# Each 1 MB weight chunk as two transfers on their own semaphores, in a two-block transformer kernel

## The reference, cut to what matters

```python
for l in range(2):                                  # first block
    x = x + hybrid_layer(x, ...)                    # rmsnorm -> h @ w_in[l] (1024 x 3488) -> MLA attention,
                                                    # short conv, spatial gate, block attention -> y @ w_out[l]
for l in range(2):                                  # second block
    x = x + hybrid_mixer(rmsnorm(x), ...)           # h @ w_in (1024 x 2048), pooling and dilated attention, @ w_out
    if l == 0: x = x + swiglu(rmsnorm(x), wg, wu, wd)        # d_ff = 2816
    else:      x = x + moe_swiglu(rmsnorm(x), w_router, ...) # 8 experts, top 2, d_ff = 3584 each
return rmsnorm(x)
```

## Time and profile before

| | us |
|---|---|
| median of three runs | 1853.41 |
| the profiled execution's own time | 1849.0 |
| its span, first to last instruction | 1847.2 |
| PE busy | 1682.5 (91% of the span) |
| DVE busy | 1357.5 (73%) |
| ACT busy | 1055.2 (57%) |
| DMA queue of SP (q1) | 454.32 MB, 69.0% of 16 engines' span |

### The profile page before, as it was taken

The page is one execution under the profiler, slowest core; times in us unless marked ns, Lnnn a source line. Parts: engine busy times, 40 slices in busy tenths (PEclk is TensorE's granted clock), DMA queues, the critical chain, the costliest instruction groups (busy, mean ns, idle before and its releaser), DMA issues.

```text
span 1847.2 us, 21996 instructions
## 1 busy us (share of the span) xinstructions
PE 1682.5 (91%) x7707; PEld 1378.7 (75%) x7707; DVE 1357.5 (73%) x1456; ACT 1055.2 (57%) x976; POOL 18.6 (1%) x34
## 2 busy tenths in 40 slices
PE   5787977896999998669999999999999999999995
PEld 4666866775788886568888878888888888788884
DVE  4855765645644564568888888899888888888886
ACT  4333444353444445227767677777677776776773
POOL 1001000000000000000000000000000000000000
PEclk9997998897999999779999999999999999999997
DMA  9423532341544554128999999999999999999992
GB/s 320 160 91 97 175 122 69 113 144 46 160 159 146 197 189 158 51 87 307 361 369 354 345 338 366 372 355 362 326 347 366 369 362 341 345 366 367 356 348 111
DMA packets 153627, 462.59 MB, mean 250 GB/s; under 512 B 7806, under 2 KB 12172, under 8 KB 153404
## 3 DMA queue, kind: packets, MB, share of 16 engines
q1 hardware_dynamic: 151120, 454.32, 69.0%
q0 software_dynamic: 1696, 5.08, 1.0%
q10 hardware_dynamic: 716, 1.85, 0.3%
HBM read 460.18 MB, written 1.05 MB: 250 GB/s over the span
## 4 chain that ended last, share of the span: by engine, by line
PE 79%; DVE 10%; issue 4%; ACT 3%; DVEq 2%; DMA 1%; ACTq 0%; SPq 0%
PE ps L1875 15%; PE ps L1877 15%; PE ps L1876 15%; PE ps L1506 8%; PE ps L1508 8%; PE ps L1507 8%; PE ps L1902 2%; DVE actv_sb L1458 2%; DMA raw_sb<-w_in 1%; PE ps L1531 1%; PE ps L1809 1%; DVE wlo_sb L850 1%; ACT whi_sb L595 1%; ACT whi_sb L602 1%; PE ps L1823 1%
## 5 line engine op out<-in xcount | busy, mean ns | idle before, releaser
L857 DVE TENSOR_TENSOR wlo_sb<-raw_sb,whi_sb 128x2048 fp32r<-128x2048 f32 x336 | 766.4, 2291 | 131.8 <-ACT whi_sb L602 130.8
L602 ACT ACTIVATE whi_sb<-raw_sb 128x2048 fp32r<-128x2048 f32 x336 | 643.6, 1918 | 271.4 <-PE ps L1877 271.4
L850 DVE TENSOR_TENSOR wlo_sb<-raw_sb,whi_sb 128x1024 fp32r<-128x1024 f32 (+2 forms) x198 | 225.5, 1181 | 178.3 <-ACT whi_sb L595 176.2
L1875 PE MATMUL ps<-whi_sb,xlo_sb 128*128 128x512 f32 x896 | 352.5, 393 | 3.9 <-DVE wlo_sb L857 1.7
L1877 PE MATMUL ps<-whi_sb,xhi_sb 128*128 128x512 f32 x896 | 349.1, 390 | 0.0
L1876 PE MATMUL ps<-wlo_sb,xhi_sb 128*128 128x512 f32 x896 | 348.8, 389 | 0.0
L595 ACT ACTIVATE whi_sb<-raw_sb 128x1024 fp32r<-128x1024 f32 (+2 forms) x198 | 192.1, 1020 | 253.6 <-PE ps L1508 239.4
L1506 PE MATMUL ps<-whi_sb,xlo_sb 128*128 128x512 f32 (+2 forms) x672 | 269.5, 401 | 22.9 <-DVE xlo_sb L895 6.1
L1507 PE MATMUL ps<-wlo_sb,xhi_sb 128*128 128x512 f32 (+2 forms) x672 | 262.8, 391 | 0.0
L1508 PE MATMUL ps<-whi_sb,xhi_sb 128*128 128x512 f32 (+2 forms) x672 | 262.4, 391 | 0.0
L1875 PEld LDWEIGHTS ps<-whi_sb,xlo_sb 128*128 128x128 f32 x896 | 168.2, 188 | 40.9 <-DVE wlo_sb L857 3.7
(11 more groups left out here) (299 smaller groups left out, 1321.8 us busy)
## 6 DMA issues: line engine op xcount, KB each, us to landing
raw_sb<-moe_wg SPq DMA_DIRECT2D x115, 1024.0 KB, 6.1
raw_sb<-moe_wu SPq DMA_DIRECT2D x112, 1024.0 KB, 6.3
raw_sb<-moe_wd SPq DMA_DIRECT2D x112, 1024.0 KB, 6.5
raw_sb<-w_in SPq DMA_DIRECT2D x40, 1024.0 KB, 5.1
raw_sb<-w_out SPq DMA_DIRECT2D x16, 1024.0 KB, 5.0
raw_sb<-ffn_wg SPq DMA_DIRECT2D x10, 1024.0 KB, 5.1
raw_sb<-ffn_wu SPq DMA_DIRECT2D x10, 1024.0 KB, 5.1
raw_sb<-ffn_wd SPq DMA_DIRECT2D x10, 1024.0 KB, 5.0
```

The costliest lines, as they stand in the source:

```text
L602: nc.scalar.activation(whi[i % SPLIT][:, :, :], raw[i % RAW][:, :, :], ACT.Copy).then_inc(hi_ready, 2)
L850: op = V.tensor_tensor(wlo[i % SPLIT][:, c:c + k // 2, 0:n], raw[i % RAW][:, c:c + k // 2, 0:n], whi[i % SPLIT][:, c:c + k // 2, 0:n], ALU ...
L857: V.tensor_tensor(wlo[i % SPLIT][:, :, :], raw[i % RAW][:, :, :], whi[i % SPLIT][:, :, :], ALU.subtract).then_inc(lo_ready, 1)
L1875: mm(out, lo, whi[q % SPLIT][:, w, :], start=first, stop=False)
```

## The change

Every chunk is now fetched by two DMAs of half the row tiles each (two row tiles of 512 columns, or one of 1024 columns; one of 512 for the last chunks of the dense feed-forward's down projection). There are twelve semaphores instead of six, one for each half of each buffer. SP waits once for the buffer and then issues both halves back to back. In `act_hi` the wait for `split_used` now comes first, and then ahead of each half copy a wait for that half's semaphore. `act_hi_whole` waits for both halves, then for `split_used`, and copies the chunk whole as before. Nothing of DVE's or PE's program is changed.

```diff
-        raw_landed = [sem(f"raw_landed{i}") for i in range(RAW)]
+        raw_landed = [sem(f"raw_landed{i}_{c}") for i in range(RAW) for c in range(2)]
...
                 sp.wait_ge(lo_ready, number(c0, i - RAW + 1, per, l))
-            sp.dma_start(wide(raw[i % RAW]) if chunk.n == WIDE else raw[i % RAW][:, 0:chunk.k, 0:chunk.n],
-                         src(chunk.k0 * PART, chunk.k * PART, chunk.n0, chunk.n)).then_inc(raw_landed[i % RAW], 16)
+            dst = wide(raw[i % RAW]) if chunk.n == WIDE else raw[i % RAW][:, 0:chunk.k, 0:chunk.n]
+            half = chunk.k // 2
+            for c in (0, half):
+                sp.dma_start(dst[:, c:c + half, :], src((chunk.k0 + c) * PART, half * PART, chunk.n0, chunk.n)).then_inc(
+                    raw_landed[2 * (i % RAW) + (1 if c else 0)], 16)
...
-            act.wait_ge(raw_landed[i % RAW], landed(c0, i, per, l))
             if not (isinstance(l, int) and c0 + i + per * l < SPLIT):
 
                 act.wait_ge(split_used, number(c0, i - SPLIT + 1, per, l))
             for c in range(0, k, k // 2):
-
+                act.wait_ge(raw_landed[2 * (i % RAW) + (1 if c else 0)], landed(c0, i, per, l))
                 nc.scalar.activation(whi[i % SPLIT][:, c:c + k // 2, 0:n], raw[i % RAW][:, c:c + k // 2, 0:n],
                                      ACT.Copy).then_inc(hi_ready, 1)
...
-            act.wait_ge(raw_landed[i % RAW], landed(AT_MOE, i, PER, l))
+            for c in range(2):
+                act.wait_ge(raw_landed[2 * (i % RAW) + c], landed(AT_MOE, i, PER, l))
             act.wait_ge(split_used, number(AT_MOE, i - SPLIT + 1, PER, l))
```

## The result

| | before | after |
|---|---|---|
| median of 13 runs each, us | 1851.48 | 1858.42 |
| lowest to highest, us | 1844.83 to 1856.52 | 1854.41 to 1862.63 |
| profiled execution / its span, us | 1849.0 / 1847.2 | 1854.41 / 1852.6 |

The changed kernel is slower: ratio 1.0036, 95% interval 1.0027 to 1.0045. The prediction was 1852.3 us (1847.3 to 1857.0), no change. It was wrong in its sign and its range.

What follows compares the result with a forecast made beforehand. The prediction took PE to bound the expert stage (busy 99.5%), with weights waited for only at the start. A 1.14 us gain there and costs of 0 elsewhere gave 1853.41 - 1.14 = 1852.3 us, range 1847.3 to 1857.

Steps and rivals of the forecast that it cites:

- Where the change can act: Whole kernel: ACT waits for transfers in three copies only, 14.2 us, in the first 27 us; a gain only there.
- The start, 1.14 us: Third chunk at the start: DVE subtracts its first half earlier, ends at 29.14 not 30.28; PE's third chunk at 32.94.
- its second chunk would start 1.15 us earlier: PE at the start: DVE ends the second chunk at 26.42 with halves, so PE starts and finishes it 1.15 us earlier.
- The second wait inside the copy, 0: ACT's `act_hi`, 99 chunks: a fulfilled wait between the half copies doesn't break their overlap; cost 0, upper end +0.8 us.
- SP issues two DMAs per chunk ... Cost 0: Expert stage, SP: two issues take 0.75 us of a 2.80 us period; SP waits 726.9 of 920 us for buffers.
- A landing has time ... Cost 0: Expert stage: 12.46 us from a chunk's issue to its copy, landing takes 9.0 at most; 3.1 us left at the worst.
- The transfer rate ... I take 0: Expert stage: needs 354 GB/s on the mean, the queue moved 386 at the start; one more completion per chunk costs 0.
- Rival A: Expert loop: each added DMA takes engine time and the experts become bound by transfers; +44 us, 1897 us; chance 5%.
- a loop turn is longer than 249 us: Expert loop: a sign that would show the forecast wrong; a turn was expected to stay at 248.4 us.

Runs made afterwards that it cites:

- e4b: Kernel before, with already fulfilled waits added in SP's expert loop (432 instructions a turn, not 306); ratio 1.0026 to the kernel before, tail 899.3 us against 894.0.
- e9b: Kernel before, with 96 already fulfilled waits added ahead of SP's expert loop, its 306 instructions kept; ratio 1.0031 to the kernel before, tail 900.1 us against 894.0.
- e3: Changed kernel, with SP's expert loop over single experts, half the instructions per turn; ratio 1.0010 to the kernel before, tail 898.8 us against the changed kernel's 903.5.
- e6: Changed kernel, with both halves on one semaphore (ACT's program as before) and SP's loop over single experts; ratio 1.0019 to the kernel before, tail 899.5 us.
- e10: Kernel before, SP waiting for one more buffer ahead of the first chunk of each pair's first expert, no code added; ratio 1.0045, tail 903.1 us against 894.0.
- e14: Changed kernel, one semaphore per buffer, SP's loop over single experts, fifth and sixth chunk held back in every expert; ratio 0.9981 to the kernel before, tail 891.2 us.
- e11: Kernel before, SP holding back the fifth and sixth chunk of each pair's first expert; ratio 0.9988, again 0.9983, tail 891.1 and 891.3 us against 894.0.
- e1: Changed kernel, with halves in projections and dense feed-forward only, the experts' chunks whole again; ratio 1.0014 to the kernel before, tail 902.7 us.

## Why the prediction was wrong

- *Where the change can act* (ACT waits for transfers only at the start): right. It was then taken for all that the change can do, "everywhere else can only cost", and the costs were looked for along the data alone.
- *The start, 1.14 us*: right in mechanism, the size off: 0.62, as the last half lands 0.5 us later than the whole did. PE gained 0.3 of it there (its third chunk started at 33.81, before at 34.08). That its second chunk would start 1.15 us earlier failed: it started at 28.28, before at 27.62, because the first one ran later (from 19.55, before from 18.77), and the third then waited for the second.
- *The second wait inside the copy, 0*: held. The copies still last 1.06 us.
- **"SP issues two DMAs per chunk ... Cost 0": the step that failed.** The issue time did fit (SP's total wait for buffers fell from 726.9 to 563.3 us, and it kept 2.80 us a period). What I didn't count is that the issues are also code: 220 instructions more in a turn and 96 more ahead of the loop, and SP is late once a turn by fetching it, 2.5 to 3.1 us. e4b, e9b: 5 to 6 us by code alone; e3, e6: 4 to 5 us less without it.
- *"A landing has time ... Cost 0"*: true for ACT, and the wrong engine. The hole is harmless to ACT; its catch-up meets PE's fetch 18 us later (e10). The wait that this step lacked is PE's, on its own code. The clock adds to it.
- *"The transfer rate ... I take 0"*: the rate held (385 to 404 GB/s above); that something else waits beside the queued transfers, PE's code, was not in the sum. Halves lengthen PE's branch to 5.15 us (the median) in e6, where the five kernels with whole transfers and no code fetched have 3.93 to 4.61, with some 0.6 MB issued and not yet moved in both. e14 shows that it is this fetch; no run shows why two transfers delay it more than one whole.
- *Rival A* (fixed cost of a DMA, +44 us) named the loop's full DMAs, but not this mechanism: the total would be bytes and completions, and ScalarE would wait for transfers. It did not. The sign *"a loop turn is longer than 249 us"* is the one that came true.
- The 0.73 us wait on "issue" and the 3.7 to 5.0 us branch stood in the trace of before. A branch that lasts microseconds, where SP's and ACT's last 0.05, was to be read as a fetch. (The opposite can't be read from it: SP's branch lasts 0.05 us in the changed kernel too, where its code is fetched.)

What stays open beside that: the tail and the start together make 8.9 us, the medians 6.9 with an interval of 5.0 to 8.3.

## What to carry to other kernels

Before adding an instruction to a hardware loop, count the loop's instructions on that engine and see whether code packets move inside its turns; a body that just fits can cease to fit by its place alone. Where the largest engine must fetch its code at a back edge, look at what the transfers do in those microseconds: a prefetcher that pauses there for one or two chunks it can spare costs nothing and gave 0.12 to 0.25% here, and one that catches up there cost 0.45%. Judge such a part by a stretch that begins behind the noise (for one and the same program the tail agreed within 1 us where the ratios lay 2 us apart).

## What the hardware showed that I had not expected

- The more weight data is issued and not yet moved when PE branches, the later PE's code packet starts: 0.9 to 1.0 us into the branch with nothing queued (e11), 1.2 to 2.6 us with some 0.6 MB in whole transfers, 2.4 to 4.0 with 0.9 to 1.1 MB (e1, e4b, e9b), and 3.4 to 3.7 us with 1.35 to 1.39 MB (e10; 1.35 MB at the 408 GB/s of that stretch are 3.3 us). The amount is not all: the ranges overlap, and halves start it later than whole transfers do (2.7 to 2.9 us with 0.6 MB in e6). The Trainium skill, "DMA: Bandwidth & Descriptors", section "Queues, rings and completion order", says that an engine takes turns between its queue rows packet by packet. By that alone the code would wait for no more than the packets being drained; no trace shows how much such a packet holds here, so whether the code stands behind all that is queued or behind a part of it stays open.
- The granted clock fell to 0.50 behind 2.6 to 2.7 us of idle PE in each turn of the changed kernel, for some 3 us, and stayed at 1.00 behind 0.73 us before. The length of the idle alone doesn't decide it: in e10's second turn it stayed at 1.00 behind 2.54 us, in e4b's first it fell to 0.50 behind 1.97 us.
